# Two-block network on one Trainium2 core: recurrent-convolution sums in PSUM, a shared tap bank, and a later start for GpSimd's taps

## The chip, the cores and the metric

One core of a Trainium2 chip runs the whole kernel in one launch. The metric is the device time of one execution in microseconds (us). Three runs of the kernel before gave 1054.37 us at the median, between 1052.43 and 1056.21.

## What is computed

x is a sequence of 256 positions with 1024 channels, held as 8 chunks of 128 channels (chunk on the partitions, positions along the free axis). A first network with two layers (pooling mixer, attention, two MLPs) runs over it, and then the second network, in which the change lies:

```
h = rmsnorm(x);  z = h @ w_in + b_in;  z_glu, z_rx, z_rg, z_ga, z_gb = split(z)
u  = z_glu[:, :1024] * sigmoid(z_glu[:, 1024:])
u  = silu(layernorm(depthwise_conv(u, 31 taps)));        y_a = u @ conv_w_out + b
xb = depthwise_conv(z_rx, 4 taps)                        # 1280 channels = 10 chunks
r, i = sigmoid(blockdiag(xb, wa) + ba), sigmoid(blockdiag(xb, wx) + bx)
a = exp(-8 * r * softplus(-lam));  hb = scan(h = a*h + sqrt(1-a*a) * i * xb)
y_b = (hb * gelu(z_rg)) @ lru_w_out
x = x + (sigmoid(z_ga) * y_a + sigmoid(z_gb) * y_b) @ w_mix
x = x + (silu(h2 @ w1) * (h2 @ w3)) @ w2;  return rmsnorm(x)
```

All of it is float32.

## The kernel before

**The weight stream.** Weights come in units of eight 128x128 tiles, two units to a DMA of 1 MB (`raw`, four slots). A unit of most phases is split into a high and a low part: ScalarE writes `w_hi` (L1080), VectorE writes `w_lo` = raw - w_hi (L1441, both inputs in SBUF, 1024 elements a partition), and TensorE does three matmuls a tile (hi by hi and hi by lo at L628 and L629, lo by hi at L634). ScalarE splits four units ahead of TensorE and VectorE three. The phases in "native" form (`rg`, `gb`, `ga` at L960, `lru` at L1009) multiply `raw` directly and need no split.

**The phases around the change**, in TensorE's order: `glu` (16 units), `rx` (10), `rg` (10, native), `gates` (8 units with 52 tiles), `gb` and `ga` (8 and 8, native), `lru` (10, native), `conv`. Their outputs go to PSUM banks 0 to 3 in turn, and a bank must have been read before unit v+4 takes it: by VectorE for `rx` (`scaled`, L1814), by ScalarE for `rg`, `gates`, `gb` and `ga` (L1287, L1352).

**The order of work is written by hand.** Each engine runs through step numbers v. In `rx`/`rg` VectorE has steps 0 to 19: for v < 10 `scaled`, then a split; from 10 on only splits (the last three of them, v = 17 to 19, are for gates units 0 to 2); then `xb_low` for the chunk whose `REC_AT` is v-1, `recurrent_conv` for the chunk whose `REC_AT` is v, and some taps of the 31-tap convolution. `REC_AT` is 1, 3, 5, 7, 9, 10, 11, 12, 13, 14. The taps per step are 3 and 0 in turn for v < 10, then 4 for five steps, 8 for two, and 5 for three; in `gates` 3 for five steps (each with a split) and 5 for three; 65 remain for `gb`/`ga`.

**The recurrent convolution of chunk m.** ScalarE writes z_rx to `rx[:, m]` (L1282) and the first product with the bias to `newt[:, m % 2]` in SBUF (`recurrent_first`, L1303). VectorE adds two taps in place in `newt` (L1821, each linked to the next by a semaphore) and writes the sum with the fourth back over `rx` (L1822). ScalarE copies `rx` to `act_hi` (`xb_high`, L1291), and VectorE writes `act_lo` = rx - act_hi (`low`, L1829). TensorE's gates need `act_hi` and `act_lo`. The recurrence later multiplies `ig` by the whole of `rx` (L1918), waits for ScalarE's decays and squares (L1922), multiplies by ScalarE's square root (L1925) and runs ten scans (L1911).

**The 31-tap convolution of u.** Chunks 0 to 5 belong to VectorE: ScalarE writes the first product (`first_tap`, L1296), VectorE adds 30 taps in place (L1845), two chunks at a time in turn. Their sums lie in PSUM, the pairs in banks 4, 5 and 7; the last tap of each writes `y` in SBUF. Chunks 6 and 7 belong to GpSimd (`pool_product` L600, `pool_add` L608, all in SBUF, 512 elements a partition, 30 of each). It begins when all eight first products are there. When all taps are done, VectorE sums `y` over chunks (L1955), and TensorE's statistics matmul on that sum stands behind the third `lru` unit; VectorE goes on with the mean at L1959.

**Banks.** Banks 4 and 5 are called `s_banks` in the rows, the others `bank`. Bank 6 held the statistics of the norm ahead of `glu` and is not touched again before the statistics in `lru`.

Of the kernel before, what the change touches and what calls it, by code (L numbers as in the profile page):

```python
# [8 lines left out]
ALU = mybir.AluOpType  # L9
ACT = mybir.ActivationFunctionType  # L10
# [14 lines left out]
TAPS, RTAPS = 31, 4  # L25
# [23 lines left out]
U0, B0, T0, A0, NATIVE = {}, {}, {}, {}, set()  # L49
# [161 lines left out]
def build(nc, weights, w_mod, w_dots, c_row, x_in, vectors, rel_bias, buckets, inv_count, identity, out):  # L211
    scratch = nc.dram_tensor("bias_by_distance", [HEADS, 384], F32, kind="Internal").ap()
    with ExitStack() as ctx:
        def sb(name, shape, dt=F32, where=ctx):
            return where.enter_context(nc.sbuf_tensor(name, shape, dt))

        def sem(name):
            return ctx.enter_context(nc.semaphore(name))
# [29 lines left out]
        newt = sb("newt", [P, 2, SEQ])  # L248
# [49 lines left out]
        with ExitStack() as part:  # L298
            RXW = SEQ + RTAPS - 1
            UW = SEQ + TAPS - 1  # L300
            rx = sb("rx", [P, RC, RXW], F32, part)
            with ExitStack() as inner:
                half_line("act", inner)
                act_hi = sb("act_hi", [P, RC, SEQ], F32R, inner)
# [3 lines left out]
            u = sb("u", [P, DC, UW], F32, part)  # L308
            y = sb("y", [P, DC, SEQ], F32, part)
# [15 lines left out]
        s_banks = ctx.enter_context(nc.psum_tensor("s_banks", [P, 2, 512], F32))  # L325
        banks = four + [s_banks[:, e, :] for e in range(2)] + [ctx.enter_context(nc.psum_tensor(f"bank{b}", [P, 512], F32)) for b in (6, 7)]
        row_banks, col_bank, pool_bank, stat_bank = (banks[4], banks[6]), banks[5], banks[7], banks[6]
        tap_banks = (banks[4], banks[5], banks[7])
        v_bank, t_banks, o_bank = banks[6], (banks[7], banks[6]), banks[3]


# [3 lines left out]
        pe_units = sem("pe_units")  # L335
# [52 lines left out]
        xb_done = sem("xb_done")  # L388
        act_hi_done = sem("act_hi_done")
        act_lo_done = sem("act_lo_done")  # L390
        h32_done = sem("h32_done")
        h32_moved = sem("h32_moved")
        rtap_done = sem("rtap_done")
        ytap_done = sem("ytap_done")
        u_done = sem("u_done")
        tap_done = sem("tap_done")
        pool_tap, pool_mult = sem("pool_tap"), sem("pool_mult")
        act_read = sem("act_read")
        decay_done = sem("decay_done")
# [9 lines left out]
        def col(name, k, n=1):  # L409

            return vec[:, VEC[name] + k:VEC[name] + k + n]
# [166 lines left out]
        @block.gpsimd  # L578
        def _(pool):
            nc.gpsimd.memset(cz[:], 0.0).then_inc(consts, 1)  # L580
            nc.gpsimd.memset(ones[:], 1.0).then_inc(consts, 1)
            nc.gpsimd.memset(rstd[:, SEQ:SEQ + 2], 1.0).then_inc(consts, 1)

            pool.wait_ge(consts, 3)
            nc.gpsimd.memset(rbx[32:33, :], -1e30).then_inc(consts, 1)
            pool.wait_ge(consts, 4)
            for t in (h_pad, s2, s4, s8):
                nc.gpsimd.memset(t[:, :, 0:16], 0.0).then_inc(consts, 1)

# [12 lines left out]
            def pool_add(k):

                pool.wait_ge(pool_mult, k)
                if k > 1:
                    pool.wait_ge(pool_tap, k - 1)
                dst = y[:, DC - POOL_TAPS:DC, :]
                nc.gpsimd.tensor_tensor(dst, dst, pool_prod[:, k % 2, :, :], ALU.add).then_inc(pool_tap, 1)  # L608

            pool.wait_ge(ytap_done, DC)  # L610
            pool_product(1)
            for k in range(1, TAPS):
                if k + 1 < TAPS:
                    pool_product(k + 1)
                pool_add(k)
# [451 lines left out]
        def _(act):  # L1067
# [220 lines left out]

            def xb_high(m):
                act.wait_ge(xb_done, m + 1)  # L1290
                act.activation(act_hi[:, m, :], rx[:, m, RTAPS - 1:], ACT.Copy).then_inc(act_hi_done, 1)  # L1291

            def first_tap(m):

                act.wait_ge(u_done, m + 1)
                act.activation(tap_sum(m), u[:, m, 0:SEQ], ACT.Identity, bias=col("dw_b", m), scale=col("dw_w", m)).then_inc(ytap_done, 1)  # L1296

            def recurrent_first(m):

                if m >= 2:  # L1300
                    act.wait_ge(xb_done, m - 1)
                act.wait_ge(z_done, 8 + m + 1)
                act.activation(newt[:, m % 2, :], rx[:, m, 0:SEQ], ACT.Identity, bias=col("rb", m), scale=col("rw", m)).then_inc(rtap_done, 1)  # L1303

            for v in range(16):
                m = v // 2
# [6 lines left out]
                if v % 2 == 1:  # L1313
                    if m >= 2:
                        act.wait_ge(u_done, m - 1)
                    if v < GLU_SPLIT:
                        act.wait_ge(tile_read, T0["glu"] + v + 1)
                        src = ab[:, 1, 0:SEQ]
                    else:
                        act.wait_ge(pe_units, U0["glu"] + v + 1)  # L1320
                        src = out_bank("glu", v)[:, 0:SEQ]
# [26 lines left out]
            for v in range(GATE_UNITS):  # L1348
                while g < 20 and GATE_DONE[g] == v:
                    m, which = g // 2, g % 2  # L1350
                    act.wait_ge(pe_units, U0["gates"] + v + 1)
                    act.activation((rt, ig)[which][:, m, :], out_bank("gates", g)[:, 0:SEQ], ACT.Sigmoid,  # L1352
                                   bias=col(("ba", "bx")[which], m)).then_inc(act_read, 1)
# [70 lines left out]
        def _(ve):  # L1424
            chain = [0]

            def link(ins):

                chain[0] += 1
                ins.then_inc(dve, 1)  # L1430
                ve.wait_ge(dve, chain[0])
# [384 lines left out]
            def recurrent_conv(m):  # L1816

                ve.wait_ge(rtap_done, m + 1)
                t = newt[:, m % 2, :]
                for k in (1, 2):  # L1820
                    link(ve.scalar_tensor_tensor(t, rx[:, m, k:k + SEQ], col("rw", RC * k + m), t, ALU.mult, ALU.add))  # L1821
                ve.scalar_tensor_tensor(rx[:, m, 3:3 + SEQ], rx[:, m, 3:3 + SEQ], col("rw", RC * 3 + m), t, ALU.mult, ALU.add)\  # L1822
                    .then_inc(xb_done, 1)

            def low(n, m, src, ready):

                ve.wait_ge(*ready)
                ve.wait_ge(act_hi_done, n + 1)
                ve.tensor_tensor(act_lo[:, m, :], src, act_hi[:, m, :].bitcast(F32), ALU.subtract).then_inc(act_lo_done, 1)  # L1829

            def xb_low(m):
                low(m, m, rx[:, m, 3:3 + SEQ], (xb_done, m + 1))

            def taps(n0, n1):


                for n in range(n0, min(n1, LAST_TAPS)):
                    pair, k, m = n // (2 * (TAPS - 1)), n % (2 * (TAPS - 1)) // 2 + 1, n % 2
                    m += 2 * pair
                    if k == 1:  # L1840
                        ve.wait_ge(ytap_done, 2 * pair + 2)
                    else:
                        ve.wait_ge(tap_done, n - 1)
                    dst = y[:, m, :] if k == TAPS - 1 else tap_sum(m)
                    ve.scalar_tensor_tensor(dst, u[:, m, k:k + SEQ], col("dw_w", DC * k + m), tap_sum(m), ALU.mult, ALU.add)\  # L1845
                        .then_inc(tap_done, 1)

            done = [0]
# [1 line left out]
            def more_taps(n):  # L1850
                taps(done[0], done[0] + n)
                done[0] += n

            for v in range(16):
                m = v // 2
# [24 lines left out]
                if v % 2 == 1:  # L1880
# [3 lines left out]
                    src = ab[:, 0, 0:SEQ] if v < GLU_SPLIT else out_bank("glu", v - 1)[:, 0:SEQ]  # L1884
# [30 lines left out]
            for v in range(16):  # L1915
                if v == 0:
                    ve.wait_ge(act_read, A0["gates"] + 20)
                    link(ve.tensor_tensor(ig[:], ig[:], rx[:, :, RTAPS - 1:], ALU.mult))  # L1918
                if v == MULT_AT:

                    ve.wait_ge(decay_done, 2 * RC + 1)
                    ve.scalar_tensor_tensor(rt[:], a2[:], 1.0, rt[:], ALU.add, ALU.mult).then_inc(mult2_done, 1)  # L1922
                if v == MULT_AT + 2:
                    ve.wait_ge(mult_done, 1)
                    link(ve.tensor_tensor(ig[:], ig[:], rt[:], ALU.mult))  # L1925
                more_taps(TAPS_AT["gb"][v])
# [258 lines left out]
```

## Time and profile before

| | us |
|---|---|
| profiled execution, its own time | 1052.81 |
| its span | 1051.0 |
| median of the three runs | 1054.37 |
| TensorE busy in the span | 993.4 (95%) |
| VectorE busy | 797.6 (76%) |
| ScalarE busy | 552.6 (53%) |
| GpSimd busy | 80.4 (8%) |
| all of VectorE's splits, L1441, 276 instructions | 337.8, mean 1230 ns |

The profile covers one execution. Busy TensorE counts matmuls as long as they are in flight, so a stretch can be "busy" at nearly full share and still be slow; the number of matmuls in a stretch tells more. Times in the timeline count from the span's start. Where one line stands for several instructions (x3), the duration runs from the first's start to the last's end; an instruction of VectorE often starts a little before the one ahead of it has ended.

### The profile page before, as it was taken

The numbers are of one execution on the slowest core, as the hardware profiler recorded it, in microseconds if no ns is written. First come the engines' busy times: TensorE is split into PE (matmuls) and PEld (weight loads), VectorE is DVE, ScalarE is ACT, GpSimd is POOL, SyncE is SP. The second block draws the span as 40 slices with busy tenths as digits, with TensorE's granted clock in tenths as the row PEclk, the third lists the DMA queues.
The fourth block names the chain that finished last, engine by engine and source line by source line (L and its number), as shares of the span: only waits on it lengthen the run. The fifth ranks groups of instructions, "written<-read, shape, count | busy, mean of one in ns | idle before, by whom it ended". The sixth has DMA issues, their size and how long they took to land.

```text
span 1051.0 us, 20066 instructions
## 1 busy us (share of the span) xinstructions
PE 993.4 (95%) x7914; PEld 941.1 (90%) x7914; DVE 797.6 (76%) x1337; ACT 552.6 (53%) x905; POOL 80.4 (8%) x74
## 2 busy tenths in 40 slices
PE   4799999999999999999999988669999999999996
PEld 2579899999998899999999987569889999999996
DVE  4767977878777687668667998999957787777554
ACT  3347675444665577874445642247306565444342
POOL 0000000000000000000000079930000000000000
PEclk9699999999999999999999999899999999999999
DMA  9997897885555665554554533234444555555531
GB/s 379 421 419 304 304 378 277 347 339 168 180 180 180 252 236 198 170 197 161 195 204 161 192 130 120 80 128 170 147 156 170 197 196 201 198 169 192 201 121 41
DMA packets 35882, 222.30 MB, mean 212 GB/s; under 512 B 3883, under 2 KB 9180, under 8 KB 9436
## 3 DMA queue, kind: packets, MB, share of 16 engines
q1 hardware_dynamic: 35804, 221.22, 58.5%
q8 instruction: 54, 0.88, 0.3%
q14 instruction: 24, 0.20, 0.0%
HBM read 220.13 MB, written 1.07 MB: 210 GB/s over the span
## 4 chain that ended last, share of the span: by engine, by line
PE 78%; DVE 12%; ACT 3%; DMA 3%; issue 2%; SPq 0%; DVEq 0%; ACTq 0%
PE bank L628 22%; PE bank L634 21%; PE bank L629 21%; PE bank L960 5%; PE bank L1009 2%; DVE newt L1821 2%; DVE w_lo L1441 2%; DMA mod_raw<-w_mod 2%; DVE s_banks L1845 2%; PE s_banks L657 1%; DVE act_lo L1829 1%; ACT w_hi L1080 1%; PE s_banks L1009 1%; DVE rx L1822 1%; DMA raw<-weights 1%
## 5 line engine op out<-in xcount | busy, mean ns | idle before, releaser
L1441 DVE TENSOR_TENSOR w_lo<-raw,w_hi 128x1024 fp32r<-128x1024 f32 x276 | 337.8, 1230 | 34.1 <-ACT w_hi L1080 31.6
L1080 ACT ACTIVATE w_hi<-raw 128x1024 fp32r<-128x1024 f32 x276 | 288.3, 1050 | 111.5 <-PE bank L634 105.2
L628 PE MATMUL bank<-xg_hi,w_hi 128*128 128x258 f32 (+1 forms) x1312 | 325.5, 285 | 1.3 <-DVE w_lo L1441 0.8
L629 PE MATMUL bank<-xg_lo,w_hi 128*128 128x258 f32 (+1 forms) x1312 | 321.1, 281 | 0.0
L628 PEld LDWEIGHTS bank<-xg_hi,w_hi 128*128 128x128 f32 x1312 | 247.6, 189 | 6.0 <-issue 4.9
L629 PEld LDWEIGHTS bank<-xg_lo,w_hi 128*128 128x128 f32 x1312 | 248.0, 189 | 0.2
L634 PE MATMUL bank<-xg_hi,w_lo 128*128 128x258 f32 (+1 forms) x1312 | 189.8, 283 | 7.5 <-DVE w_lo L1441 7.5
L634 PEld LDWEIGHTS bank<-xg_hi,w_lo 128*128 128x128 f32 x1312 | 170.4, 189 | 8.6 <-DVE w_lo L1441 8.3
L628 PE MATMUL bank<-hid_hi,w_hi 128*128 128x256 f32 x512 | 123.5, 279 | 0.0
L629 PE MATMUL bank<-hid_lo,w_hi 128*128 128x256 f32 x512 | 123.4, 279 | 0.0
L629 PEld LDWEIGHTS bank<-hid_lo,w_hi 128*128 128x128 f32 x512 | 96.0, 188 | 0.0
L628 PEld LDWEIGHTS bank<-hid_hi,w_hi 128*128 128x128 f32 x512 | 96.0, 188 | 0.0
L634 PE MATMUL bank<-hid_hi,w_lo 128*128 128x256 f32 x512 | 70.7, 279 | 0.0
L634 PEld LDWEIGHTS bank<-hid_hi,w_lo 128*128 128x128 f32 x512 | 64.8, 188 | 0.0
L960 PE MATMUL bank<-h32b,raw 128*128 128x256 f32 x256 | 55.4, 379 | 0.0
L960 PEld LDWEIGHTS bank<-h32b,raw 128*128 128x128 f32 x256 | 48.6, 190 | 6.6
L1181 ACT ACTIVATE ub<-ab 128x256 f32<-128x256 f32 x64 | 32.6, 509 | 37.6 <-DVE ab L1629 37.5
L960 PE MATMUL bank<-sga,raw 128*128 128x256 f32 x160 | 39.5, 407 | 11.0 <-ACT grg L1287 11.0
L1492 DVE CUSTOM_DVE_ANT_0 mod_raw<-mod_raw,c_all,vec 128x1024 f32<-128x1024 f32 x40 | 49.6, 1276 | 0.0
L960 PEld LDWEIGHTS bank<-sga,raw 128*128 128x128 f32 x160 | 32.0, 204 | 18.2 <-issue 13.5
L1845 DVE SCALAR_TENSOR_TENSOR s_banks<-u,vec,s_banks 128x256 f32<-128x256 f32 x116 | 48.2, 477 | 0.0
L608 POOL TENSOR_TENSOR y<-y,pool_prod 128x512 f32<-128x512 f32 x30 | 45.5, 1516 | 0.1
(243 smaller groups left out, 1389.7 us busy)
## 6 DMA issues: line engine op xcount, KB each, us to landing
raw<-weights SPq DMA_DIRECT2D x157, 1024.0 KB, 5.0
mod_raw<-w_mod SPq DMA_DIRECT2D x28, 1024.0 KB, 11.2
mod_raw<-w_dots SPq DMA_DIRECT2D x20, 1024.0 KB, 8.8
toep<-bias_by_distance SPq DMA_DIRECT2D x8, 256.0 KB, 5.4
x<-x_in SPq DMA_DIRECT2D x1, 1024.0 KB, 5.0
toep<-bias_by_distance SPq DMA_DIRECT2D x8, 128.0 KB, 3.8
y_out<-yout SPq DMA_DIRECT2D x4, 256.0 KB, 2.4
c_all<-c_row SPq DMA_DIRECT2D x1, 512.0 KB, 15.0
```

The costliest lines, as they stand in the source:

```text
L608: nc.gpsimd.tensor_tensor(dst, dst, pool_prod[:, k % 2, :, :], ALU.add).then_inc(pool_tap, 1)
L628: pe.matmul(dst, hi, r_hi, start=start, stop=False, skip_group_check=True)
L629: pe.matmul(dst, hi, r_lo, start=False, stop=False, skip_group_check=True)
L634: return pe.matmul(dst, lo, r_hi, start=False, stop=stop, skip_group_check=True)
L960: mm = pe.matmul(out_bank(name, v)[:, 0:SEQ], raw[:, slot, ((at % 2) * UT + k) * P:((at % 2) * UT + k + 1) * P], src[:, k, 0:SEQ], start=k ...
L1009: mm = pe.matmul(out_bank("lru", m)[:, 0:SEQ], raw[:, slot, ((at % 2) * UT + s) * P:((at % 2) * UT + s + 1) * P], rt[:, k, :], start=k == ...
L1080: act.activation(pool_w_hi[:, at, :] if name == "pool" and at < 2 else w_hi[:, at % HL, :], raw[:, slot, (at % 2) * UT * P:(at % 2 + 1) * ...
L1181: act.activation(ub[:, j % 2, :], ab[:, j % 2, 0:SEQ], ACT.Relu, bias=ab[:, j % 2, SEQ:SEQ + 1]).then_inc(relu_done, 1)
L1441: ve.tensor_tensor(lo, raw[:, slot, (at % 2) * UT * P:(at % 2 + 1) * UT * P], hi.bitcast(F32), ALU.subtract).then_inc(lo_done, 1)
L1492: ve.tensor_tensor_reduce(w, w, c_all[:], 1.0, col("b_mod", at + half), ALU.mult, ALU.add, accum_out=modv[:, at + half:at + half + 1]).the ...
L1821: link(ve.scalar_tensor_tensor(t, rx[:, m, k:k + SEQ], col("rw", RC * k + m), t, ALU.mult, ALU.add))
L1845: ve.scalar_tensor_tensor(dst, u[:, m, k:k + SEQ], col("dw_w", DC * k + m), tap_sum(m), ALU.mult, ALU.add)\
```

## The change

The first part puts the running sum of the recurrent convolution into PSUM: `rec_sum(m)` is the first half of bank 7 or bank 6 by the parity of m. VectorE's three taps all work in place there. ScalarE copies the finished sum twice, to `rx` and to `act_hi`. `low` reads the sum from PSUM. Since `act_lo` now is the last reader of that bank, `recurrent_first(m)` waits for the `act_lo` of m-2 where it waited for the sum of m-2. The multiplication at L1918 waits for the ten copies to `rx`.

The second part frees bank 7: the third pair of chunks sums in bank 4, which the first pair used. Its first products go to `y` in SBUF until then, and its first tap (k = 1) reads `y` and writes bank 4; that tap now waits for the tap two before it, as all others do.

The third part makes GpSimd wait for the end of the last `rx` unit on TensorE before its first product.

```diff
-        tap_banks = (banks[4], banks[5], banks[7])
+        tap_banks = (banks[4], banks[5], banks[4])
+        rec_banks = (banks[7], banks[6])
...
+        rx_done = sem("rx_done")
...
+        def first_sum(m):
+            return y[:, m, :] if m >= 4 else tap_sum(m)
+        def rec_sum(m):
+            return rec_banks[m % 2][:, 0:SEQ]
...
             pool.wait_ge(ytap_done, DC)
+            pool.wait_ge(pe_units, U0["rg"])
             pool_product(1)
...
             def xb_high(m):
                 act.wait_ge(xb_done, m + 1)
-                act.activation(act_hi[:, m, :], rx[:, m, RTAPS - 1:], ACT.Copy).then_inc(act_hi_done, 1)
+                act.activation(rx[:, m, RTAPS - 1:], rec_sum(m), ACT.Copy).then_inc(rx_done, 1)
+                act.activation(act_hi[:, m, :], rec_sum(m), ACT.Copy).then_inc(act_hi_done, 1)
             def first_tap(m):
-                act.activation(tap_sum(m), u[:, m, 0:SEQ], ACT.Identity, bias=..., scale=...)
+                act.activation(first_sum(m), u[:, m, 0:SEQ], ACT.Identity, bias=..., scale=...)
             def recurrent_first(m):
                 if m >= 2:
-                    act.wait_ge(xb_done, m - 1)
+                    act.wait_ge(act_lo_done, m - 1)
                 act.wait_ge(z_done, 8 + m + 1)
-                act.activation(newt[:, m % 2, :], rx[:, m, 0:SEQ], ...)
+                act.activation(rec_sum(m), rx[:, m, 0:SEQ], ...)
...
             def recurrent_conv(m):
                 ve.wait_ge(rtap_done, m + 1)
-                t = newt[:, m % 2, :]
+                t = rec_sum(m)
                 for k in (1, 2):
                     link(ve.scalar_tensor_tensor(t, rx[:, m, k:k + SEQ], col("rw", RC * k + m), t, ALU.mult, ALU.add))
-                ve.scalar_tensor_tensor(rx[:, m, 3:3 + SEQ], rx[:, m, 3:3 + SEQ], col("rw", RC * 3 + m), t, ALU.mult, ALU.add)\
+                ve.scalar_tensor_tensor(t, rx[:, m, 3:3 + SEQ], col("rw", RC * 3 + m), t, ALU.mult, ALU.add)\
                     .then_inc(xb_done, 1)
...
             def xb_low(m):
-                low(m, m, rx[:, m, 3:3 + SEQ], (xb_done, m + 1))
+                low(m, m, rec_sum(m), (xb_done, m + 1))
...
                     if k == 1:
                         ve.wait_ge(ytap_done, 2 * pair + 2)
-                    else:
+                    if n > 1:
                         ve.wait_ge(tap_done, n - 1)
                     dst = y[:, m, :] if k == TAPS - 1 else tap_sum(m)
-                    ve.scalar_tensor_tensor(dst, u[:, m, k:k + SEQ], col("dw_w", DC * k + m), tap_sum(m), ALU.mult, ALU.add)
+                    src = first_sum(m) if k == 1 else tap_sum(m)
+                    ve.scalar_tensor_tensor(dst, u[:, m, k:k + SEQ], col("dw_w", DC * k + m), src, ALU.mult, ALU.add)
...
                     ve.wait_ge(act_read, A0["gates"] + 20)
+                    ve.wait_ge(rx_done, RC)
                     link(ve.tensor_tensor(ig[:], ig[:], rx[:, :, RTAPS - 1:], ALU.mult))
```

## Rows read from the trace of the kernel before

**Rows 1.** Windows: busy PE, PEld, DVE, ACT, POOL; then PE clock, DMA share, GB/s
```profile
609.00:634.50 25.50, 22.04 (x186) 21.63 (x184) 25.25 (x30) 10.44 (x18) 23.05 (x17) 1.00 0.36 124
...
657.00:693.00 36.00, 25.18 (x96) 20.10 (x96) 35.10 (x49) 12.49 (x25) 33.60 (x28) 0.91 0.26 88
693.00:719.20 26.20, 20.57 (x157) 20.21 (x158) 26.20 (x52) 13.33 (x24) 0.00 (x0) 0.93 0.53 178
719.20:774.40 55.20, 55.20 (x257) 48.58 (x257) 53.41 (x100) 25.76 (x44) 0.00 (x0) 1.00 0.43 145
```

**Rows 2.** Waits between 609 and 720 us: total, times, longest
```profile
ACT act_hi L1291 <- DVE rx L1822: 24.8, 6, 5.3
...
PE bank L960 <- ACT grg L1287: 11.0, 5, 3.9
...
PE bank L634 <- DVE w_lo L1441: 7.2, 3, 2.9
```

**Rows 3.** TensorE's timeline (start, duration): the end of rx unit 6, the start of unit 7
```profile
624.97 1.11 PE L634 MATMUL bank<-xg_hi,w_lo 128*128 128x256 f32 x8
625.91 0.28 PE L628 MATMUL bank<-xg_hi,w_hi 128*128 128x256 f32 x1
```

**Rows 4.** VectorE's timeline: `scaled` of rx units 1, 2 and 4
```profile
612.09 0.43 DVE L1814 TENSOR_TENSOR ab<-bank,rstd 128x256 f32<-128x256 f32 x1
...
618.00 0.41 DVE L1814 TENSOR_TENSOR ab<-bank,rstd 128x256 f32<-128x256 f32 x1
...
628.45 0.41 DVE L1814 TENSOR_TENSOR ab<-bank,rstd 128x256 f32<-128x256 f32 x1
```

**Rows 5.** Groups by line on VectorE while GpSimd works, 611 to 692 us
```profile
L1821 DVE SCALAR_TENSOR_TENSOR newt<-rx,vec,newt 128x256 f32<-128x256 f32 x20 | 25.8, 1288 | 2.5 <-ACT newt L1303 2.1
L1845 DVE SCALAR_TENSOR_TENSOR s_banks<-u,vec,s_banks 128x256 f32<-128x256 f32 x39 | 16.2, 476 | 0.0
...
L1829 DVE TENSOR_TENSOR act_lo<-rx,act_hi 128x256 fp32r<-128x256 f32 x10 | 11.0, 1096 | 1.5 <-ACT act_hi L1291 1.5
L1441 DVE TENSOR_TENSOR w_lo<-raw,w_hi 128x1024 fp32r<-128x1024 f32 x6 | 10.7, 1785 | 0.0
```

**Rows 6.** Groups by line on ScalarE in the same stretch
```profile
L1303 ACT ACTIVATE newt<-rx,vec 128x256 f32<-128x256 f32 x10 | 5.9, 586 | 0.0
...
L1291 ACT ACTIVATE act_hi<-rx 128x256 fp32r<-128x256 f32 x10 | 4.1, 410 | 24.8 <-DVE rx L1822 24.8
...
L1338 ACT ACTIVATE h32b<-sga 128x2048 f32<-128x2048 f32 x1 | 1.9, 1896 | 0.0
```

**Rows 7.** VectorE's timeline with GpSimd idle, after 692 us
```profile
696.81 1.21 DVE L1441 TENSOR_TENSOR w_lo<-raw,w_hi 128x1024 fp32r<-128x1024 f32 x1
697.95 2.04 DVE L1845 SCALAR_TENSOR_TENSOR s_banks<-u,vec,s_banks 128x256 f32<-128x256 f32 x5
...
771.44 1.66 DVE L1934 SCALAR_TENSOR_TENSOR x<-x,vec,rstd 128x256 f32<-128x256 f32 x4
...
797.34 0.43 DVE L1446 TENSOR_TENSOR newt<-newt 128x256 f32<-128x256 f32 x1 [0.86 <-ACT newt L1099]
797.80 0.42 DVE L1447 SCALAR_TENSOR_TENSOR newt<-newt,var 128x256 f32<-128x256 f32 x1
```

**Rows 8.** VectorE's timeline in the recurrence and the statistics
```profile
723.53 2.81 DVE L1918 TENSOR_TENSOR ig<-ig,rx 128x2560 f32<-128x2560 f32 x1
...
767.85 3.67 DVE L1955 TENSOR_REDUCE acc<-y 128x256 f32<-128x2048 f32 x1
...
785.25 0.42 DVE L1959 TENSOR_SCALAR newt<-bank 128x256 f32<-128x256 f32 x1 [12.15 <-PE bank L686]
```

**Rows 9.** ScalarE's timeline: first read of a gb bank behind the square root
```profile
741.91 0.47 ACT L1287 ACTIVATE sgb<-bank,vec 128x256 f32<-128x256 f32 x1
```

**Rows 10.** GpSimd's timeline: its first and its last instructions
```profile
610.90 2.04 POOL L600 TENSOR_TENSOR pool_prod<-u,vec 128x512 f32<-128x512 f32 x2 [50.14 <-ACT y L1296]
...
689.07 2.69 POOL L608 TENSOR_TENSOR y<-y,pool_prod 128x512 f32<-128x512 f32 x2
```

More of the change, by code:

```diff
@@ L1290, in xb_high @@
                 act.wait_ge(xb_done, m + 1)
-                act.activation(act_hi[:, m, :], rx[:, m, RTAPS - 1:], ACT.Copy).then_inc(act_hi_done, 1)
+                act.activation(rx[:, m, RTAPS - 1:], rec_sum(m), ACT.Copy).then_inc(rx_done, 1)
+                act.activation(act_hi[:, m, :], rec_sum(m), ACT.Copy).then_inc(act_hi_done, 1)
             def first_tap(m):
                 act.wait_ge(u_done, m + 1)
-                act.activation(tap_sum(m), u[:, m, 0:SEQ], ACT.Identity, bias=col("dw_b", m), scale=col("dw_w", m)).then_inc(ytap_done, 1)
+                act.activation(first_sum(m), u[:, m, 0:SEQ], ACT.Identity, bias=col("dw_b", m), scale=col("dw_w", m)).then_inc(ytap_done, 1)
             def recurrent_first(m):
                 if m >= 2:
-                    act.wait_ge(xb_done, m - 1)
+                    act.wait_ge(act_lo_done, m - 1)
                 act.wait_ge(z_done, 8 + m + 1)
-                act.activation(newt[:, m % 2, :], rx[:, m, 0:SEQ], ACT.Identity, bias=col("rb", m), scale=col("rw", m)).then_inc(rtap_done, 1)
+                act.activation(rec_sum(m), rx[:, m, 0:SEQ], ACT.Identity, bias=col("rb", m), scale=col("rw", m)).then_inc(rtap_done, 1)
             for v in range(16):
@@ L1841, in taps @@
                         ve.wait_ge(ytap_done, 2 * pair + 2)
-                    else:
+                    if n > 1:
                         ve.wait_ge(tap_done, n - 1)
                     dst = y[:, m, :] if k == TAPS - 1 else tap_sum(m)
-                    ve.scalar_tensor_tensor(dst, u[:, m, k:k + SEQ], col("dw_w", DC * k + m), tap_sum(m), ALU.mult, ALU.add)\
+                    src = first_sum(m) if k == 1 else tap_sum(m)
+                    ve.scalar_tensor_tensor(dst, u[:, m, k:k + SEQ], col("dw_w", DC * k + m), src, ALU.mult, ALU.add)\
                         .then_inc(tap_done, 1)
```

## The prediction

> **What bounds the kernel now.** I began with the busy time by stretch [rows 1], because the page gives TensorE 95% and hides where it idles. From 609 to 693 us VectorE is busy nearly all the time (25.25 of 25.5, 35.10 of 36.0 us), and so is GpSimd, while TensorE has 96 matmul records in 36 us (two a native tile, so six units) at a mean clock of 0.91. From 719.2 us TensorE alone sets the pace: 16 native units in 55.2 us, 3.45 us each, at clock 1.00. The waits come next [rows 2]: TensorE waits 11.0 us for ScalarE to read rg's banks, ScalarE itself waits 24.8 us for VectorE's recurrent sums, and 7.2 us of TensorE's waits are for VectorE's splits. So VectorE is the bound between 628 and 719 us. Its timeline says how slow: two rx units take 10.45 us [rows 4], where TensorE needs 2.82 each (eight matmuls start in 625.91 - 624.97 = 0.94 us, 0.1175 apiece, and a unit has 24) [rows 3].
>
> Then the price of each kind of VectorE instruction, with GpSimd working [rows 5] and idle [rows 7]. The tap with one input in SBUF and one in PSUM takes 0.476 us in both. The split, two inputs in SBUF, takes 1.785 against 1.21. The recurrent taps, two inputs in SBUF, take 1.288, though a linked operation of that size in SBUF takes 0.42 when GpSimd is idle. `act_lo`, two inputs in SBUF, takes 1.096. So what is slow is not the arithmetic: two-SBUF-input instructions wait for GpSimd. The Trainium skill, "SBUF — State Buffer", section "Who interferes with whom", states this rule: with two SBUF inputs VectorE contends with a GpSimd instruction that reads SBUF, the loser being blocked for a whole instruction, and with one it doesn't. By that rule, the trace agrees.
>
> **Prices after.** The start-to-start intervals, GpSimd idle [rows 7]: split 1.14, tap (2.04-0.48)/4 = 0.39, linked operation its duration + 0.03.
> - Recurrent taps: one SBUF input, so the taps' price, linked twice: 2 x 0.51 + 0.39 = 1.4 us a chunk in place of about 3.9 (3 x 1.29). Bounds for one operation: 0.39 (unlinked tap) and 1.29 (nothing gained); I take the tap's, the same form on the same kinds of memory.
> - `act_lo`: one SBUF input, 0.35 in place of 1.05 (bounds 0.35 and 1.1).
> - A split with GpSimd idle: 0.58 less than beside it.
> - A rule against the change: SBUF and PSUM operands cost the same here, taps in PSUM start 0.39 apart and four of the same form all in SBUF (1.66-0.48)/3 = 0.39 [rows 7]; the sum counts nothing for it. The Trainium skill, "VectorE: DVE Perf Modes", section "Rules for kernel authors", advises to copy a PSUM result to SBUF if many operations follow, and its errata section gives a PSUM source 62 cycles more at 0.96 GHz; by that the 30 taps would cost some 2 us more (an estimate from that page). The measurement decides.
> - ScalarE: a second copy a chunk, 0.41, some 0.33 start to start. Behind it are the first product of the next chunk (0.59) and an rg read [rows 6].
>
> **rx.** Last undisturbed, TensorE is at unit 6, whose low matmuls run at 624.97 [rows 3]. A VectorE step without a recurrent tap now is 0.34 + 1.14 + 0.35 + 1.18 (three taps) + about 0.2 wait for the later `act_hi` = 3.2; one with is 0.34 + 1.14 + 1.4 = 2.9. That is 6.1 for two units, where TensorE takes 5.64; from step 1 at 612.1 [rows 4] VectorE reaches step 6 at 627.2 and writes the last rx split by 628.7, before TensorE wants it (633.4). So TensorE finishes rx without a wait: 624.97 + 0.94 + 3 x 2.82 = 634.4. VectorE's steps 7 to 9 have no split and so wait for ScalarE (1.5 + 1.4; 1.7 + 1.53; 1.5 + 1.4): it is at 639.4 when they end.
>
> **rg.** TensorE: ten units of 3.45, no bank late (rg unit 2 needs the read of rx unit 8 at 633.7; unit 4 needs ScalarE's first rg read, about 643): 634.4 + 34.5 = 668.9, also at full clock, since it no longer idles. VectorE: in step 10 the two copies stand behind ScalarE's 1.9 us copy of h32 [rows 6] and end 1.2 after the sum; with `act_lo`, the wait for the next first product, 1.4 and 1.6 of taps that is 4.7; steps 11 to 14 at 0.35 + 1.4 + 1.57 = 3.3; steps 15 and 16 at 3.5 and 3.15: 639.4 + 4.7 + 13.3 + 6.7 = 664.1. ScalarE has 1.9 us of work in each 3.3, and delivers the next first product 1.4 us after a sum, inside the 1.6 of taps: no wait.
>
> **Gates.** GpSimd starts at 634.4, so the eight gates' splits now lie beside it, where before they did not: 1.14 + 0.58 = 1.72 each (bounds 1.14, and 1.14 + 1.45, a whole GpSimd addition). Split 0 ends at 664.1 + 1.7 = 665.8, 1 and 2 each 3.7 later (5 taps), 3 another 3.7, 4 to 7 each 2.9 (3 taps): the last at 688.4. TensorE needs 2.3 us a unit (52 tiles x 3 matmuls x 0.1175 = 18.3), starts at 668.9, and waits from the fourth on for VectorE. End: 688.4 + 2.3 = 690.7, against 719.2 now: **28.5 us earlier**. With no lock at all TensorE's own pace would end it at 687.2 (32.0 earlier).
>
> **gb, ga and the rest.** TensorE runs 55.2 us of native work with weights at 145 GB/s [rows 1], so the queue has room. What could hold it is a bank: ga's first unit needs ScalarE's read of gb's fifth, now at 741.91 [rows 9], 4.9 us before its use at 719.2 + 27.6 = 746.8. Of the 18 taps behind the last split none is dearer, so L1918 moves by 28 us to 695.5. Locks on L1918 and L1922 (0.7 each) and on the two taps k = 1 whose source now is `y` (together up to 2.0) put L1922's end about 3.5 us later in relation: 1.4 us of slack are left. GpSimd took 81 us [rows 10], so it ends near 634.4 + 81 + 3 = 719, and L1955 wants it near 744. VectorE arrives there about 5 us later in relation, and has 12.15 us of idle time in front of L1959 [rows 8] to lose. The other additions (waits for `rx_done`, for the tap two back, first products to `y` instead of bank 7) end long before they are asked for: nothing. If that cover goes, one split's 1.14 us is the size. All behind ga moves as a block.
>
> **Sum.** 1052.81 - 28.5 = 1024.3 in the profiled execution's terms; its time lies 1.6 below the median of the runs, on which it would be 1025.9. I give 1025.
>
> **Rivals.**
> 1. The lock costs more in the gates: each of eight splits waits a whole addition (1.45 instead of 0.58), 7 us, and the late L1922 makes ga wait 1.5: gain 20, **1033**. For it: the recurrent taps now lose 0.87 each. Against it: the splits, at 1.785, lose 0.58 beside the same GpSimd work. By the same section on interference a block is for the whole of the other's instruction, which would give up to 1.45 here.
> 2. ScalarE becomes the wait: the chain sum, two copies, next first product, comes late in each of the six chunks of rg and by 0.5 in four of rx, about 1 us each: gain 21, **1032**. For it: ScalarE already waits at each hand-over [rows 2]; against it, the 1.6 us of taps between.
> 3. The sums gain nothing where they are: slow because of the chain on one buffer, not of GpSimd. Then 30 taps and ten `act_lo` stay as they are, rx's six splits give back 3.5, the gates' eight splits take 4.6, ScalarE's second copy 1.5: **1055.5**, slower by 2.6. It decides from a price of about 1.2 us a recurrent tap upward. Against it: 0.476 for the same form in the same stretch [rows 5], and 0.42 for linked operations without GpSimd [rows 7].
> 4. VectorE's chain to the square root holds ga for some 4 us: **1028**.
>
> **Chances.** Forecast (gain 25 to 32) 0.70; rival 1 0.12; rival 2 0.11; rival 4 0.05; rival 3 0.02. Range 1020 (no lock on the splits, TensorE's pace) to 1035 (rivals 1 and 2, a little worse). A measurement here can tell 0.3%, 3 us, from no change: faster 0.97, same 0.01, slower 0.02.
>
> **What would show it.** L1821 and L1822's successors near 0.48 us, `act_lo` 0.42, rx's splits 1.21, gates' splits near 1.8; the two rx units between VectorE's `scaled` 6 us apart; rg's first matmul near 634.5, gb's near 691; GpSimd from 634 to about 719; TensorE's clock 1.00 through rg. Recurrent taps over 0.9 us, or gb's first matmul after 699, would make it wrong.

## The result and the profile after

The changed kernel takes 1024.64 us at the median of four runs (1024.02 to 1026.65), against 1054.07 for the kernel before in the runs now known (1052.43 to 1056.21). The ratio is 0.9723, with a 95% interval from 0.9701 to 0.9745: 29 us faster. The forecast was 1025.

The profiled execution was the slowest of the four, 1026.65 us with a span of 1024.9, and its gain on the one shown before is 26.2 us. The two differ ahead of `rx` too, where they run the same instructions: ScalarE's first `rx` write starts at 609.75 us there and at 612.87 here, and over the ten profiles of this case, of nine kernels that differ only behind this point, it lies between 609.65 and 613.57. So the times below are compared from this write on. Lines of the changed file are some 10 to 14 higher, so an instruction of before is found under another number: the splits are L1453, the recurrent taps L1833 and L1834, `act_lo` L1841, ScalarE's copies L1302 and L1303, native matmuls L971, GpSimd's L610 and L618.

The windows of the changed kernel, columns as in [rows 1]:

```profile
609.00:634.50 25.50, 25.50 (x219) 25.50 (x219) 23.81 (x45) 15.08 (x27) 0.00 (x0) 1.00 0.56 184
634.50:669.00 34.50, 34.50 (x173) 30.73 (x173) 30.63 (x73) 16.85 (x36) 30.22 (x27) 1.00 0.38 134
669.00:692.00 23.00, 21.35 (x164) 20.20 (x163) 23.00 (x36) 14.56 (x26) 22.45 (x15) 1.00 0.55 195
692.00:747.00 55.00, 55.00 (x261) 48.54 (x260) 54.53 (x99) 25.68 (x44) 30.73 (x20) 1.00 0.44 152
```

In the first two stretches TensorE has no gap (22.04 of 25.50 and 25.18 of 36.00 in [rows 1]), and in the second VectorE has 3.9 us of idle time. The granted clock is 1.00 throughout, where it was 0.91 in rg and 0.93 in the gates. GpSimd's work has moved behind 634.5 us. In the third stretch VectorE is full and TensorE short by 1.65 us: the gates are what VectorE still holds. VectorE's groups by line from 612 to 692 us:

```profile
L1858 DVE SCALAR_TENSOR_TENSOR s_banks<-u,vec,s_banks 128x256 f32<-128x256 f32 x81 | 33.6, 480 | 0.0
L1453 DVE TENSOR_TENSOR w_lo<-raw,w_hi 128x1024 fp32r<-128x1024 f32 x15 | 22.5, 1500 | 0.0
L1833 DVE SCALAR_TENSOR_TENSOR bank<-rx,vec,bank 128x256 f32<-128x256 f32 x20 | 9.7, 487 | 2.4 <-ACT bank L1315 2.1
L1834 DVE SCALAR_TENSOR_TENSOR bank<-rx,vec,bank 128x256 f32<-128x256 f32 x10 | 4.9, 490 | 0.3
L1841 DVE TENSOR_TENSOR act_lo<-bank,act_hi 128x256 fp32r<-128x256 f32 x10 | 4.2, 422 | 2.3 <-ACT act_hi L1303 2.1
```

Against [rows 5], L1833's twenty taps take 9.7 us instead of 25.8, the ten `act_lo` 4.2 instead of 11.0, and the 31-tap convolution's taps cost what they did. One idle entry is longer: VectorE waits 2.1 us for ScalarE's later `act_hi`, where it was 1.5.

The gates, seen from VectorE (timeline, splits only) and from GpSimd (timeline):

```profile
666.58 1.41 DVE L1453 TENSOR_TENSOR w_lo<-raw,w_hi 128x1024 fp32r<-128x1024 f32 x1
...
676.32 1.36 DVE L1453 TENSOR_TENSOR w_lo<-raw,w_hi 128x1024 fp32r<-128x1024 f32 x1
...
678.77 2.14 DVE L1453 TENSOR_TENSOR w_lo<-raw,w_hi 128x1024 fp32r<-128x1024 f32 x1
...
688.47 2.13 DVE L1453 TENSOR_TENSOR w_lo<-raw,w_hi 128x1024 fp32r<-128x1024 f32 x1
```
```profile
676.67 1.91 POOL L610 TENSOR_TENSOR pool_prod<-u,vec 128x512 f32<-128x512 f32 x1
678.54 1.29 POOL L618 TENSOR_TENSOR y<-y,pool_prod 128x512 f32<-128x512 f32 x1
679.91 1.90 POOL L610 TENSOR_TENSOR pool_prod<-u,vec 128x512 f32<-128x512 f32 x1
```

The first four splits take 1.33 to 1.41 us, the last four 2.13 or 2.14, where 1.21 is the price alone. The one at 678.77 meets the addition that began at 678.54; that one ends at 679.83, and the split, 1.1 us behind it, at 680.91. The product issued at 679.91 then waits for the split and takes 1.90 instead of 1.04. Both engines now repeat in 3.2 us, so each of the last splits meets an addition at the same point. The first four meet the end of a GpSimd instruction instead: there five taps lie between two splits, from 676.32 on only three.

### The profile page after: what moved, and what is told of

It reads as the page before. It is cut to its first block, busy times and chain, and to the rows that moved or that the text cites. A ratio compares the mean times of both kernels' runs of the same rounds, so it can differ in the third digit from the quotient of the medians.

```text
span 1024.9 us, 20081 instructions
## 1 busy us (share of the span) xinstructions
PE 984.2 (96%) x7914; PEld 937.5 (91%) x7914; DVE 771.1 (75%) x1337; ACT 555.1 (54%) x915; POOL 85.3 (8%) x74
## 4 chain that ended last, share of the span: by engine, by line
PE 80%; DVE 11%; ACT 4%; DMA 3%; issue 2%; DVEq 0%; SPq 0%; ACTq 0%
PE bank L639 22%; PE bank L645 22%; PE bank L640 22%; PE bank L971 5%; DVE w_lo L1453 3%; DVE s_banks L1858 3%; PE bank L1020 3%; PE s_banks L668 1%; DMA mod_raw<-w_mod 1%; ACT w_hi L1091 1%; DMA raw<-weights 1%; PE s_banks L1020 1%; DVE bank L1833 1%; DVE mod_raw L1504 1%; ACT ub L1192 1%
## 5 line engine op out<-in xcount | busy, mean ns | idle before, releaser
L1453 DVE TENSOR_TENSOR w_lo<-raw,w_hi 128x1024 fp32r<-128x1024 f32 x276 | 339.0, 1234 | 35.1 <-ACT w_hi L1091 32.7
L1858 DVE SCALAR_TENSOR_TENSOR s_banks<-u,vec,s_banks 128x256 f32<-128x256 f32 x172 | 71.2, 480 | 0.2
L971 PE MATMUL bank<-h32b,raw 128*128 128x256 f32 x256 | 55.4, 379 | 0.0
L971 PEld LDWEIGHTS bank<-h32b,raw 128*128 128x128 f32 x256 | 48.6, 190 | 6.6
L1192 ACT ACTIVATE ub<-ab 128x256 f32<-128x256 f32 x64 | 32.6, 509 | 37.7 <-DVE ab L1641 37.6
L610 POOL TENSOR_TENSOR pool_prod<-u,vec 128x512 f32<-128x512 f32 x30 | 43.4, 1447 | 76.2 <-PE bank L645 74.0
L1648 DVE TENSOR_TENSOR hid_lo<-sb,hid_hi 128x256 fp32r<-128x256 f32 (+1 forms) x64 | 27.3, 426 | 23.6 <-ACT sb L1195 22.8
```

The lines of the kernel that those rows point to most:

```text
L971: mm = pe.matmul(out_bank(name, v)[:, 0:SEQ], raw[:, slot, ((at % 2) * UT + k) * P:((at % 2) * UT + k + 1) * P], src[:, k, 0:SEQ], start=k ...
L1192: act.activation(ub[:, j % 2, :], ab[:, j % 2, 0:SEQ], ACT.Relu, bias=ab[:, j % 2, SEQ:SEQ + 1]).then_inc(relu_done, 1)
L1453: ve.tensor_tensor(lo, raw[:, slot, (at % 2) * UT * P:(at % 2 + 1) * UT * P], hi.bitcast(F32), ALU.subtract).then_inc(lo_done, 1)
L1648: ve.tensor_tensor(chunk(hid_lo, t), sb2[:, j % 2, :], chunk(hid_hi, t).bitcast(F32), ALU.subtract).then_inc(hid_lo_done, 1)
```

## The experiments

All run from the two kernels; the first four beside each other, the last four too. The table gives medians, and from each profile the stretch from ScalarE's first `rx` write to gb's first matmul, which holds the change and is free of what varies ahead of it; from gb on, before and after take the same (1051.0 - 719.01 = 332.0 and 1024.9 - 692.87 = 332.0 us). Something varies behind it too. Seven of the ten profiles take 332.0 us from gb on, but e2 takes 1038.9 - 709.20 = 329.7 and e6 takes 1024.6 - 694.90 = 329.7: in these two and in e7 the matmuls of the last product (`@ w2`) start 0.113 us apart, in the others 0.118. The windows of after_again and then of e6 show it, at the same granted clock; why is open. The medians hold both this and what varies ahead, so a difference of 2 or 3 us is read from the stretch.

```profile
980.00:1010.00 30.00, 30.00 (x257) 30.00 (x257) 16.21 (x24) 14.56 (x23) 0.00 (x0) 1.00 0.16 58
...
980.00:1010.00 30.00, 30.00 (x267) 30.00 (x267) 17.05 (x23) 14.54 (x24) 0.00 (x0) 1.00 0.21 71
```

| kernel | sums in | GpSimd's start | median us | ratio to before | first rx write to gb |
|---|---|---|---|---|---|
| before | SBUF | 610.9 | 1054.3 / 1053.9 | | 719.01 - 609.75 = 109.3 |
| after | PSUM | end of rx | 1024.64; again 1026.20 | 0.9723; 0.9738 | 692.87 - 612.87 = 80.0 |
| e1_early | PSUM | 614.3 | 1026.44 | 0.9739 | 694.80 - 613.18 = 81.6 |
| e2_late_only | SBUF | end of rx | 1040.56 | 0.9878 | 709.20 - 612.24 = 97.0 |
| e3_before_no_pool | SBUF | none | 1022.75 | 0.9695 | 689.36 - 611.84 = 77.5 |
| e4_after_no_pool | PSUM | none | 1022.76 | 0.9712 | 687.28 - 609.65 = 77.6 |
| e5_pause | PSUM | end of rx, pause | 1021.71 | 0.9699 | 687.23 - 609.89 = 77.3 |
| e6_rx_by_vector | PSUM, last in rx | end of rx | 1026.41 | 0.9733 | 694.90 - 613.57 = 81.3 |
| e7_start_gates | PSUM | end of rg | 1033.20 | 0.9810 | 692.49 - 612.37 = 80.1 |

### after_again: the measure for the second four

> The changed kernel once more, as the measure for the runs beside it: 1024.6 us, within 2.

Measured: 1026.20 us (1025.12 to 1026.75, five runs), ratio 0.9738 with an interval from 0.9717 to 0.9758; the stretch is 80.0 us again. e5, e6 and e7 are set against this run.

### e1_early: the sums in PSUM alone

```diff
             pool.wait_ge(ytap_done, DC)
-            pool.wait_ge(pe_units, U0["rg"])
             pool_product(1)
```

> The changed kernel, with GpSimd starting its taps as early as in the kernel before (beside rx). Theory (the sums' place is worth nearly all, because VectorE's instructions with one SBUF input do not wait for GpSimd; the later start only saves some 0.6 us on each of rx's six splits, and these stay ahead of TensorE): rx still ends without a wait, VectorE reaches the gates' splits about 3.5 us later, some of the last of those run with GpSimd idle; about 3 us slower than the changed kernel, 1027.5 us. Rival (the later start carries a large part of the gain): 1035 to 1045 us. Recurrent taps stay at 0.49 us under the theory.

Measured: 1026.44 us (1026.27 to 1028.62), ratio 0.9739 with an interval from 0.9708 to 0.9771. The medians do not tell it from the changed kernel (1024.64 and 1026.20); the stretch does. By the stretch, the sums alone bring 27.6 of the 29.3 us, and the later start the last 1.6, not 3. The taps are at 0.485 us with GpSimd beside them; the splits of rx rise to 1.60 to 1.67, as they were, and TensorE does not notice, for the first rg matmul is 637.80 - 613.18 = 24.62 us behind the first `rx` write, the same 24.62 as in the changed kernel (637.49 - 612.87). Groups of VectorE in rx, then the gates' splits of its timeline:

```profile
L1452 DVE TENSOR_TENSOR w_lo<-raw,w_hi 128x1024 fp32r<-128x1024 f32 x7 | 11.0, 1572 | 0.0
L1832 DVE SCALAR_TENSOR_TENSOR bank<-rx,vec,bank 128x256 f32<-128x256 f32 x8 | 3.9, 485 | 1.2 <-ACT bank L1314 1.0
...
681.61 1.21 DVE L1452 TENSOR_TENSOR w_lo<-raw,w_hi 128x1024 fp32r<-128x1024 f32 x1
683.91 2.14 DVE L1452 TENSOR_TENSOR w_lo<-raw,w_hi 128x1024 fp32r<-128x1024 f32 x1
```

I had expected the gates' splits to be partly free of GpSimd. It ends at 698.4, so all eight lie beside it, and they cost 13.5 us against 14.0 in the changed kernel. The later start saves VectorE 2.5 us on rx's splits. Of these 2.1 are left at the first split of the gates (668.94 - 613.18 = 55.8 us behind the first `rx` write, against 666.58 - 612.87 = 53.7), and the gates' splits, cheaper in e1, take back 0.5, which leaves the 1.6.

### e2_late_only: the later start alone

```diff
 (in the kernel before)
             pool.wait_ge(ytap_done, DC)
+            pool.wait_ge(pe_units, U0["rg"])
             pool_product(1)
```

> The kernel before, with only the later start of GpSimd; the sums stay in SBUF. Theory: up to the end of rx on TensorE the recurrent taps take 0.42 to 0.48 us, behind it 1.3 again, for six or seven of the ten chunks, and act_lo 1.1: 17 to 20 us slower than the changed kernel, 1044 us. Rival (chained sums in SBUF are slow by themselves): taps at 1.29 us from the start, near 1052 us.

Measured: 1040.56 us (1039.06 to 1043.62) where 1044 was expected, ratio 0.9878 (0.9841 to 0.9916); the stretch is 17.0 us longer than in the changed kernel. The same instruction in the same kernel, first with GpSimd idle (612 to 637 us), then with it at work (641 to 683 us):

```profile
L1822 DVE SCALAR_TENSOR_TENSOR newt<-rx,vec,newt 128x256 f32<-128x256 f32 x8 | 3.9, 485 | 1.2 <-ACT newt L1304 1.1
L1823 DVE SCALAR_TENSOR_TENSOR rx<-rx,vec,newt 128x256 f32<-128x256 f32 x4 | 1.9, 486 | 0.1
...
L1822 DVE SCALAR_TENSOR_TENSOR newt<-rx,vec,newt 128x256 f32<-128x256 f32 x11 | 14.3, 1298 | 0.2
L1823 DVE SCALAR_TENSOR_TENSOR rx<-rx,vec,newt 128x256 f32<-128x256 f32 x6 | 7.8, 1296 | 0.2
```

0.485 becomes 1.298. The chain in SBUF is not slow by itself; GpSimd makes it so. The two parts overlap: alone they bring 27.6 and 12.3 us, together 29.3.

### e3_before_no_pool and e4_after_no_pool: no GpSimd beside it

```diff
             pool.wait_ge(ytap_done, DC)
-            pool_product(1)
-            for k in range(1, TAPS):
-                ...
             ve.wait_ge(tap_done, LAST_TAPS)
-            ve.wait_ge(pool_tap, TAPS - 1)
+            ve.wait_ge(ytap_done, DC)
```

(the same edit in the kernel before and in the changed one, where the wait for the end of rx goes too)

> The kernel before without GpSimd's 30 products and 30 additions, so chunks 6 and 7 of the 31-tap convolution hold their first product only; nothing else differs, the sums stay in SBUF. Theory (the wait is for GpSimd): recurrent taps 0.42 to 0.48 us, act_lo 0.42, splits 1.21, and TensorE alone sets the pace through rx, rg and gates: 1021 us. Rival (the chain in SBUF or the read-after-write is slow in itself): taps stay near 1.3 us and the time near 1048 us.

> The changed kernel without GpSimd's 30 products and 30 additions (chunks 6 and 7 of the 31-tap convolution hold their first product only). Theory: the eight splits of the gates take 1.21 us instead of 1.75, TensorE waits for none, 3 to 3.5 us less than the changed kernel: 1021 us, equal to the kernel before without GpSimd's taps. If PSUM operands were dearer, VectorE's recurrent taps here would be longer than there, by up to 0.065 us, with no effect on the time. Rival (ScalarE's second copy or its later hand-over holds TensorE): 1023 us or more, above the other.

Measured: 1022.75 us (1019.59 to 1023.16) and 1022.76 us (1021.06 to 1025.02), with intervals of the ratio that largely overlap (0.9660 to 0.9730, 0.9678 to 0.9746); the stretch is 77.5 and 77.6 us. With GpSimd out of the way the place of the sums makes no difference. VectorE's groups, sums in SBUF first, then sums in PSUM:

```profile
L1816 DVE SCALAR_TENSOR_TENSOR newt<-rx,vec,newt 128x256 f32<-128x256 f32 x20 | 9.7, 484 | 2.5 <-ACT newt L1298 2.1
L1817 DVE SCALAR_TENSOR_TENSOR rx<-rx,vec,newt 128x256 f32<-128x256 f32 x10 | 4.9, 485 | 0.4
L1824 DVE TENSOR_TENSOR act_lo<-rx,act_hi 128x256 fp32r<-128x256 f32 x10 | 4.2, 420 | 1.6 <-ACT act_hi L1286 1.6
```
```profile
L1827 DVE SCALAR_TENSOR_TENSOR bank<-rx,vec,bank 128x256 f32<-128x256 f32 x20 | 9.7, 486 | 2.4 <-ACT bank L1309 2.1
L1828 DVE SCALAR_TENSOR_TENSOR bank<-rx,vec,bank 128x256 f32<-128x256 f32 x10 | 4.9, 490 | 0.3
L1835 DVE TENSOR_TENSOR act_lo<-bank,act_hi 128x256 fp32r<-128x256 f32 x10 | 4.2, 421 | 2.3 <-ACT act_hi L1297 2.1
```

The price of PSUM is 1 to 5 ns an instruction. ScalarE's second copy shows as 2.3 against 1.6 us of VectorE's waits and costs nothing in the stretch. The rest, 80.0 - 77.6 = 2.4 us, is what GpSimd still takes from the changed kernel, all of it in the gates: their first matmul comes 58.97 us behind the first `rx` write in the changed kernel, in e3 and in e4 alike.

### e5_pause: GpSimd stands still during the gates

```diff
             for k in range(1, TAPS):
+                if k == 12:
+                    pool.wait_ge(lo_done, splits(U0["gates"] + 7))
                 if k + 1 < TAPS:
                     pool_product(k + 1)
```

> The changed kernel with a pause of GpSimd: behind the 11th of its 30 additions it waits until VectorE has written the last of the gates' splits. Theory: the splits take 1.21 us, TensorE waits for none, gb begins 3.5 us earlier; GpSimd ends some 20 us later than in the changed kernel, near 743, about when VectorE wants y, and there are 9 us of idle time behind that: 1021 us, 3.5 below the changed kernel. Rival (the tail of GpSimd is needed earlier than it seems, or its locks on the scans hold hb): equal to the changed kernel or slower.

Measured: 1021.71 us (1019.06 to 1024.15, five runs), ratio to before 0.9699 (0.9674 to 0.9723); the changed kernel beside it had 1026.20 and 0.9738 (0.9717 to 0.9758). The stretch is 77.3 us, what e4 has without any GpSimd work, so the pause takes back all that GpSimd cost there, 2.7 us; the medians differ by 4.5, and the two sets of runs beside each other do not overlap (1024.15 is the highest here, 1025.12 the lowest there), but only the 2.7 is carried by the profiles. It is the fastest complete kernel of this study, faster than both. GpSimd's timeline around the pause and at its end, and VectorE behind it:

```profile
660.33 1.27 POOL L618 TENSOR_TENSOR y<-y,pool_prod 128x512 f32<-128x512 f32 x1
683.41 1.04 POOL L610 TENSOR_TENSOR pool_prod<-u,vec 128x512 f32<-128x512 f32 x1 [21.81 <-DVE w_lo L1455]
...
735.23 3.07 POOL L618 TENSOR_TENSOR y<-y,pool_prod 128x512 f32<-128x512 f32 x2
```
```profile
723.63 1.12 DVE L1926 TENSOR_TENSOR_SCAN rt<-av,ig 128x256 f32<-128x256 f32 x1
724.78 1.57 DVE L1928 TENSOR_TENSOR rt<-rt,grg 128x512 f32<-128x512 f32 x1
...
741.06 0.68 DVE L1926 TENSOR_TENSOR_SCAN rt<-av,ig 128x256 f32<-128x256 f32 x1
```

The bill moves to the recurrence: scans of 0.68 us take 1.0 to 1.4 while GpSimd works. It is paid from idle time: VectorE's wait in front of the mean shrinks from 9.2 to 4.7 us.

### e6_rx_by_vector: without ScalarE's second copy

```diff
             def xb_high(m):
-                act.activation(rx[:, m, RTAPS - 1:], rec_sum(m), ACT.Copy).then_inc(rx_done, 1)
-                act.activation(act_hi[:, m, :], rec_sum(m), ACT.Copy).then_inc(act_hi_done, 1)
+                act.activation(act_hi[:, m, :], rx[:, m, RTAPS - 1:], ACT.Copy).then_inc(act_hi_done, 1)
             def recurrent_conv(m):
-                ve.scalar_tensor_tensor(t, rx[:, m, 3:3 + SEQ], ...)
+                ve.scalar_tensor_tensor(rx[:, m, 3:3 + SEQ], rx[:, m, 3:3 + SEQ], ...)
             def xb_low(m):
-                low(m, m, rec_sum(m), (xb_done, m + 1))
+                low(m, m, rx[:, m, 3:3 + SEQ], (xb_done, m + 1))
```

(with the waits of before for `recurrent_first` and L1918)

> The changed kernel with the last recurrent tap written to rx in SBUF by VectorE, as in the kernel before, so that ScalarE makes one copy and act_lo again has two inputs in SBUF; the first three sums stay in PSUM. Theory: act_lo takes 0.42 us in rx, where GpSimd is idle, and 1.1 to 1.3 in rg, six or seven times: VectorE reaches the gates' splits 4 to 5 us later, 1028.5 us. Rival (ScalarE's second copy costs more than it gives): 1024 us or less.

Measured: 1026.41 us (1022.92 to 1027.34), equal to the changed kernel beside it; the stretch is 1.3 us longer. Neither expectation is met: the direction is the theory's, the size is a third of it. `act_lo` in rg, from VectorE's timeline:

```profile
643.01 1.42 DVE L1840 TENSOR_TENSOR act_lo<-rx,act_hi 128x256 fp32r<-128x256 f32 x1 [0.68 <-ACT act_hi L1302]
...
647.36 0.61 DVE L1840 TENSOR_TENSOR act_lo<-rx,act_hi 128x256 fp32r<-128x256 f32 x1
...
650.89 0.83 DVE L1840 TENSOR_TENSOR act_lo<-rx,act_hi 128x256 fp32r<-128x256 f32 x1
```

I had taken the 1.1 us of [rows 5]. Here the first of six meets an addition near its start and loses 1.0 us; for the other five, with no instruction in front of them that waits for GpSimd, GpSimd's instruction is near its end, and they lose 0.2 to 0.4. The ten take 6.6 us instead of 4.2. Writing the sum to `rx` on ScalarE is worth 1.3 us by the stretch, too little for the medians to show.

### e7_start_gates: GpSimd another 34 us later

```diff
-            pool.wait_ge(pe_units, U0["rg"])
+            pool.wait_ge(pe_units, U0["gates"])
```

> The changed kernel with GpSimd starting at the end of rg instead of the end of rx, 34.5 us later. Theory: the gates' splits cost what they cost now; GpSimd ends near 760, its waits for VectorE included, VectorE's sum over y comes some 17 us later, 9 of them are idle time in front of the mean: about 8 us slower than the changed kernel, 1033 us. Rival (GpSimd's end has more room than the idle time shows): 1025 us.

Measured: 1033.20 us (1030.67 to 1035.80), ratio 0.9810 (0.9780 to 0.9840): 7.0 us slower than the changed kernel beside it. Below are VectorE's timeline at the sum over y, the waits from 740 to 790 us, TensorE's timeline behind the wait and the window from 760 to 768 us:

```profile
760.94 3.59 DVE L1969 TENSOR_REDUCE acc<-y 128x256 f32<-128x2048 f32 x1 [8.31 <-POOL y L618]
...
PE bank L697 <- DVE acc L1969: 6.3, 1, 6.3
...
764.58 1.22 PE L697 MATMUL bank<-acc,ones 128*128 128x256 f32 x2 [6.32 <-DVE acc L1969]
765.60 8.03 PE L1020 MATMUL bank<-rt,raw 128*128 128x256 f32 x32
...
760.00:768.00 8.00, 3.42 (x9) 2.83 (x10) 7.03 (x7) 0.00 (x0) 0.83 (x1) 0.57 0.00 0
```

The sum over y starts 16.8 us later than in the changed kernel (760.94 - 744.18), its 9.2 us of idle time are used up and TensorE waits 6.3. In the changed kernel GpSimd ends at 723.1, VectorE asks for y at 744.2 and then has 9.2 us idle: 30 us of room. Here GpSimd ends at 760.8, 37.7 later, so 7.5 are too many.

The 7.0 between the medians holds what varies elsewhere as well; the profile shows a loss of 8.0 us: from gb on it takes 1030.2 - 692.49 = 337.7, against the 329.7 of e2 and e6, whose last product ran at the same pace. 6.3 of it are the wait. The rest is the clock: the granted clock is 0.57 between 760 and 768 us, and behind the wait the two statistics matmuls take 1.22 us and the next 32 of `lru` 8.03, where the changed kernel has 0.59 and 7.07, 1.6 us more.

## Why the prediction was right

The time came out at 1024.64 for 1025, and for its reasons. Step by step, with the profile's 3.1 us of a later `rx` taken off:

| step | predicted | measured |
|---|---|---|
| recurrent tap, linked; last | 0.51; 0.39 | 0.52 (a pair 1.01 us); 0.40 |
| two rx steps of VectorE | 6.1 | 6.03 |
| rg's first matmul | 634.4 | 637.49 - 3.12 = 634.4 |
| gates' first matmul | 668.9 | 671.84 - 3.12 = 668.7 |
| gates' splits, mean | 1.79 | 14.0 / 8 = 1.75 |
| end of the last split | 688.4 | 690.60 - 3.12 = 687.5 |
| gb's first matmul | 690.7 | 692.87 - 3.12 = 689.8 |
| GpSimd's end | 719 | 723.58 - 3.12 = 720.5 |
| idle in front of the mean | 12.15 less about 5 | 9.2 |

**rx and rg.** The prediction's first claim, that instructions with two SBUF inputs wait for GpSimd and not for the arithmetic, is shown by e2, e3 and e4. Its price alone was a little low: the recurrent tap takes 0.484 us without GpSimd and not the 0.42 of [rows 7], so it lost 0.80 and not 0.87. TensorE's 11.0 us of waits for banks are gone, of the 7.2 for splits the same view shows 0.6, in the gates, and the granted clock of rg is 1.00 instead of 0.91. The gain in the stretch is 29.3 us where 28.5 was worked out.

**The gates.** The mean is right and the picture behind it was not: I took a random meeting of split and GpSimd, 0.58 us each. The eight in fact fall into step with GpSimd, four at about +0.15 and four at +0.92. The whole addition, the upper bound, is 1.27 us when nothing holds it; the 1.45 of the prediction has waits for VectorE in it. That the sum agrees (4.3 us against 4.6) is partly luck. The 3.5 us that I put on the lock are 2.4 by e4 and 2.7 by e5, since the last split ends 0.9 us sooner than worked out.

**gb and ga.** L1922's successor ends 713.67 - 692.87 = 20.8 us into gb against 19.2 before, 1.6 later and not 3.5. The bank in question was misread. ScalarE reads five of gb's units before the square root, so [rows 9] shows the sixth, whose bank ga's second unit takes. ScalarE's timeline of the kernel before, ahead of [rows 9], and then that of the changed kernel:

```profile
731.13 1.20 ACT L1287 ACTIVATE sgb<-bank,vec 128x256 f32<-128x256 f32 x3
...
734.44 0.48 ACT L1287 ACTIVATE sgb<-bank,vec 128x256 f32<-128x256 f32 x1
736.48 0.47 ACT L1287 ACTIVATE sgb<-bank,vec 128x256 f32<-128x256 f32 x1 [1.56 <-PE bank L960]
...
710.33 0.47 ACT L1298 ACTIVATE sgb<-bank,vec 128x256 f32<-128x256 f32 x1 [1.54 <-PE bank L971]
...
717.36 0.84 ACT L1298 ACTIVATE sgb<-bank,vec 128x256 f32<-128x256 f32 x2
```

In the changed kernel the sixth read starts at 717.36 and ga's second unit at 723.95, 6.6 us later (8.2 in the kernel before), where the prediction counted on 1.4. The mistake made the path look tighter than it is and did not move the sum. The two taps k = 1 that read `y` cost 0.8 us together, not 2.0.

**The rivals.** The first (every split waits a whole addition) came half true in the last four splits. The second (ScalarE becomes the wait) shows in VectorE's 2.1 us of waits for `act_hi`, 0.6 of them new, which lie in steps 8 and 10 where there was slack; e4 against e3 prices it at nothing, in a kernel without GpSimd. The third, the slower one, falls by e3: without GpSimd the taps in SBUF take 0.484. The later start was worth less than the text let one think: 1.6 us. And its risk was real, only further out: e7, 34 us later, shows it. The fourth (the chain to the square root holds ga) did not happen: `lru`'s first matmul comes 55.25 us behind gb's in both kernels.

What stays open is the share of the bank change (the third pair in bank 4), which was not run alone. It was made to free bank 7, and its one visible cost is the 0.8 us above.

## What to carry to other kernels

When VectorE and GpSimd work side by side, sort VectorE's instructions by the number of inputs in SBUF before reading their durations: those with two pay for what is left of GpSimd's instruction, here up to 1.0 us of 1.26, and a running sum moved to PSUM stops paying at once. Do that before moving GpSimd's work: here the place of the sums alone was worth 27.6 of 29.3 us, and the start of GpSimd 12.3 alone but only 1.6 on top of it. What is left is best given to GpSimd as windows: run it where VectorE has no such instruction on the path, stop it where VectorE's splits are the bound (2.7 us more here), and look at the idle time in front of the consumer before starting it late.

## What the runs showed of the hardware that I had not expected

A blocked instruction waits for the rest of the one that runs, so two engines with periodic work fall into step. VectorE's turn of a split and five taps takes 3.1 us in e3, one with three taps 2.31, and GpSimd's turn of a product and an addition takes 2.34 where nothing holds it (from 659.95 to 662.29 in the changed kernel). Beside each other both turns of VectorE, and GpSimd's, become about 3.24 us. The long turn loses 0.15 us at its split (1.35), the short one 0.92 (2.13): two taps fewer between the splits brought nothing, because VectorE only waited longer. 2.13 is found in the last splits of the changed kernel, after_again, e1, e2, e6 and e7.

Chained two-input instructions are the worst case, 1.30 us for 0.485. The rows fit one GpSimd instruction between each two of them, for two linked taps take 2.67 us and GpSimd's two instructions beside them begin 2.59 us apart. VectorE's and then GpSimd's timeline of the kernel before:

```profile
665.15 2.67 DVE L1821 SCALAR_TENSOR_TENSOR newt<-rx,vec,newt 128x256 f32<-128x256 f32 x2
...
665.03 1.10 POOL L600 TENSOR_TENSOR pool_prod<-u,vec 128x512 f32<-128x512 f32 x1
666.10 1.44 POOL L608 TENSOR_TENSOR y<-y,pool_prod 128x512 f32<-128x512 f32 x1
667.62 1.10 POOL L600 TENSOR_TENSOR pool_prod<-u,vec 128x512 f32<-128x512 f32 x1
```

The Trainium skill, "SBUF — State Buffer", section "Who interferes with whom", says that whoever issues first has the shared ports for its whole instruction and the other is fully blocked. The rows fit that, and it is less than the prediction made of it: the loser does not wait for a whole instruction but for the remainder, up to 0.92 us of an addition of 1.29 for the splits and 1.0 of 1.26 for `act_lo` in e6.

Neither engine is favoured. L1932 (L1918 before) and a product of GpSimd begin within 0.06 us of each other; VectorE's 2.81 us instruction came through untouched, and the product took 3.77 us instead of 1.04. L1936 (L1922 before) begins while a product runs and took 3.44 instead of 2.82:

```profile
697.57 2.81 DVE L1932 TENSOR_TENSOR ig<-ig,rx 128x2560 f32<-128x2560 f32 x1
710.23 3.44 DVE L1936 SCALAR_TENSOR_TENSOR rt<-a,rt 128x2560 f32<-128x2560 f32 x1
...
697.51 3.77 POOL L610 TENSOR_TENSOR pool_prod<-u,vec 128x512 f32<-128x512 f32 x1
709.95 1.04 POOL L610 TENSOR_TENSOR pool_prod<-u,vec 128x512 f32<-128x512 f32 x1
```

A tap with its sum in PSUM costs what one in SBUF does (0.486 against 0.484 us). The Trainium skill, "VectorE: DVE Perf Modes", section "The TRN2 errata", gives a PSUM source 62 cycles more, 0.065 us at 0.96 GHz (an estimate from that page). The trace does not show it for an instruction with one input in each; the measurement decides. ScalarE's copy of 256 elements is even a little shorter from PSUM: 0.36 to 0.39 us against 0.41 from SBUF [rows 6].
